# One front stage for an encoder layer on one NeuronCore: norm, input projection, forget gates and bias table merged

## Chip, core and metric

The kernel runs on one core of a Trainium2 chip, as one launch. The metric is the device time of the launch in microseconds, over repeated executions on the chip.

## What is computed

One inference step of one layer (DEPTH = 1) of a streaming encoder, for 2048 prompt rows and 8 streams of 16 new rows, so 2176 rows of 1024 values, all float32. Cut to the part that the change touches:

```python
h = rmsnorm(x, norm_mix_pre)            # x * rsqrt(mean(x*x) + 1e-6) * gain
z = h @ w_in                            # columns [qA | kA | vA | forget A (8) | qB | kB | vB], 512 each
logf = log_sigmoid(forget + b_forget)   # 8 heads
c = cumsum(logf)                        # over rows; group A adds C[t] - C[s] to its logits
# group B: chunked attention over 9 chunks of 64 with a learned bias rel_bias[h, clip(t - s)]
```

After that come the attention of both groups, the output projection and a SwiGLU feed-forward block, each with its own norm; the change leaves them alone but for what is told below. Keys, values and logf are outputs too.

## The kernel before, in words

Every float32 product is made of three float32r matmuls (`three`, L169): both operands are split into a high part (a rounded copy) and a low part (value minus high), and high x high, high x low and low x high are added up in PSUM. The work is a row of stages; each stage ends when all five engines have finished it, and a short block that clears semaphores stands ahead of the next.

- `norm_inputs` (L70) takes x, stored transposed (128 partitions x 8 feature groups x 2176 rows), in five blocks of 448 or 384 rows (`TBLK`). ScalarE squares the eight groups (L105), GpSimd adds them up (L122, L125), TensorE adds over partitions with a matrix of ones (L134), VectorE and ScalarE make 1/rms (L142, L107, L144), VectorE scales x by gain and 1/rms (L147), ScalarE copies the high part (L110) and VectorE takes the low part (L151). `xhi` and `xlo` stay in SBUF whole. There is one accumulator and the blocks follow one another.
- `project_in` (L178) takes w_in in twelve slabs of 256 columns: eight for q and k (group A and B), four for v. GpSimd makes a slab's high part (L225), VectorE its low part (L235). For q and k the slab is the stationary operand and the output is transposed: 2 x 5 groups of 24 matmuls a slab into `pz`, copied out by ScalarE (L279) and stored from ScalarE's queue. For v the rows are stationary: 17 groups of 24 matmuls a slab into `pv`, copied out at L289. The order is q and k, then v, then 120 matmuls with the 8 forget columns as stationary operand (L295 copies them out to `fT` in DRAM).
- `forget` (L304) reads fT back as 8 partitions x 2176 and runs a chain of single instructions over it, one after another: log-sigmoid (L358 to L370; ScalarE at L343 and L345), running sum (L371), sign (L372), and the running sum of the streams' stored and new values (L374, L375).
- `band_tables` (L378) reads rel_bias, extends it to 8 x 384 (L409, L410), writes it to DRAM 128 times over in eight DMAs, all from 8 partitions of SBUF (L398), and reads it back along a diagonal into `brel` (L403); two memsets on GpSimd mask its corners (L418, L420).
- `attend_prompt` (L464) begins by loading q, k, v and the bias of the first head pair (L537 to L550), splits them (L710, L712, L758, L760) and makes its first scores at L615. Its six `sums` buffers (NSM) hold the softmax sums of a job until VectorE has evicted it.

In each stage every engine has one instruction stream of its own, written out by hand, so what a stream waits for holds up all behind it. Two other stages of the kernel take 1/rms with a power on GpSimd: L1317, L1327 and L1962, `tensor_tensor(..., ALU.pow)` with an exponent of -0.5, on one or two columns of 128 partitions.

Of the kernel before, what the change touches and what calls it, by code (L numbers as in the profile page):

```python
# [9 lines left out]
ds = bass.ds  # L10
# [21 lines left out]
def f32(ap):  # L32

    return ap.bitcast(F32)
# [35 lines left out]
def norm_inputs(nc, t, xhi, xlo, keep):  # L70

    with ExitStack() as ctx:
        m = Mem(nc, ctx, "nrm", keep)
        W = 448
        x = [m.sb(f"x{u}", [P, KD, W]) for u in range(2)]
        sq = [m.sb(f"sq{u}", [P, W]) for u in range(2)]
        acc = m.sb("acc", [P, W])
        var = m.sb("var", [P, W])
        rstd = m.sb("rstd", [P, W])
        ones = m.sb("ones", [P, P])  # L80
        gain = m.sb("gain", [P, KD])
        tot = m.ps("tot", [P, 512])
        s_x = [m.sem(f"s_x{u}") for u in range(2)]
        s_gain, s_ones, s_sq, s_acc, s_tot, s_var, s_std, s_rstd, s_xn, s_hi, s_lo = (
            m.sem(n) for n in ("gain", "ones", "sq", "acc", "tot", "var", "std", "rstd", "xn", "hi", "lo"))
        with nc.Block() as block:

            @block.sync
            def _(sp):
                sp.dma_start(gain[:], t["g_pre"]).then_inc(s_gain, 16)  # L90
                for b, (t0, w) in enumerate(TBLK):
                    if b >= 2:
                        sp.wait_ge(s_lo, b - 1)
                    sp.dma_start(x[b % 2][:, :, :w], t["xT"][:, :, t0:t0 + w]).then_inc(s_x[b % 2], 16)
                sp.wait_ge(s_lo, len(TBLK))

            @block.scalar
            def _(act):
                for b, (t0, w) in enumerate(TBLK):
                    act.wait_ge(s_x[b % 2], 16 * (b // 2 + 1))  # L100
                    for k in range(KD):
                        n = b * KD + k
                        if n >= 2:
                            act.wait_ge(s_acc, n - 1)
                        nc.scalar.activation(sq[n % 2][:, :w], x[b % 2][:, k, :w], ACT.Square).then_inc(s_sq, 1)  # L105
                    act.wait_ge(s_var, b + 1)
                    nc.scalar.activation(var[:, :w], var[:, :w], ACT.Sqrt).then_inc(s_std, 1)  # L107
                    for k in range(KD):
                        act.wait_ge(s_xn, b * KD + k + 1)
                        last = nc.scalar.activation(xhi[:, k, t0:t0 + w], x[b % 2][:, k, :w], ACT.Copy)  # L110
                        last.then_inc(s_hi, 1)

            @block.gpsimd
            def _(pool):
                for b, (t0, w) in enumerate(TBLK):
                    for k in range(KD):
                        n = b * KD + k
                        pool.wait_ge(s_sq, n + 1)
                        if k == 0:
                            if b >= 1:  # L120
                                pool.wait_ge(s_tot, b)
                            nc.gpsimd.tensor_copy(acc[:, :w], sq[n % 2][:, :w]).then_inc(s_acc, 1)  # L122
                        else:
                            pool.wait_ge(s_acc, n)
                            nc.gpsimd.tensor_tensor(acc[:, :w], acc[:, :w], sq[n % 2][:, :w], ALU.add).then_inc(s_acc, 1)  # L125

            @block.tensor
            def _(pe):
                pe.wait_ge(s_ones, 1)
                for b, (t0, w) in enumerate(TBLK):  # L130
                    pe.wait_ge(s_acc, (b + 1) * KD)
                    if b >= 1:
                        pe.wait_ge(s_var, b)
                    nc.tensor.matmul(tot[:, :w], ones[:], acc[:, :w], start=True, stop=True).then_inc(s_tot, 1)  # L134

            @block.vector
            def _(dve):
                nc.vector.memset(ones[:], 1.0).then_inc(s_ones, 1)
                dve.wait_ge(s_gain, 16)
                for b, (t0, w) in enumerate(TBLK):  # L140
                    dve.wait_ge(s_tot, b + 1)
                    nc.vector.tensor_scalar(var[:, :w], tot[:, :w], 1.0 / D, EPS, ALU.mult, ALU.add).then_inc(s_var, 1)  # L142
                    dve.wait_ge(s_std, b + 1)
                    nc.vector.reciprocal(rstd[:, :w], var[:, :w]).then_inc(s_rstd, 1)  # L144
                    dve.wait_ge(s_rstd, b + 1)
                    for k in range(KD):
                        nc.vector.scalar_tensor_tensor(x[b % 2][:, k, :w], x[b % 2][:, k, :w], gain[:, k:k + 1], rstd[:, :w],  # L147
                                                       ALU.mult, ALU.mult).then_inc(s_xn, 1)
                    for k in range(KD):
                        dve.wait_ge(s_hi, b * KD + k + 1)  # L150
                        last = nc.vector.tensor_tensor(xlo[:, k, t0:t0 + w], x[b % 2][:, k, :w], f32(xhi[:, k, t0:t0 + w]),  # L151
                                                       ALU.subtract)
                    last.then_inc(s_lo, 1)


def pairs(eng, n, body):

    body(0)
    with eng.Fori(1, n) as i:
        body(i)  # L160


# [15 lines left out]
def project_in(nc, t, xhi, xlo, keep):  # L178

    CW = 256  # L180
    NZ, NV = 4 * GW // CW, 2 * GW // CW
    NS, NBK = NZ + NV, len(TBLK)
    with ExitStack() as ctx:
        m = Mem(nc, ctx, "prj", keep)
        raw = [m.sb(f"raw{u}", [P, KD, CW]) for u in range(2)]
        hi = [m.sb(f"hi{u}", [P, KD, CW], F32R) for u in range(2)]
        lo = [m.sb(f"lo{u}", [P, KD, CW], F32R) for u in range(2)]
        zo = [m.sb(f"zo{u}", [P, 448]) for u in range(NBK)]
        vo = [m.sb(f"vo{u}", [P, CW]) for u in range(2)]
        wf = m.sb("wf", [P, KD, H])  # L190
        wfh = m.sb("wfh", [P, KD, H], F32R)
        wfl = m.sb("wfl", [P, KD, H], F32R)
        pz = [m.ps(f"pz{u}", [P, 512]) for u in range(NBK)]
        pv = [m.ps(f"pv{u}", [P, 512]) for u in range(2)]
        s_raw = [m.sem(f"raw{u}") for u in range(2)]
        s_zs = [m.sem(f"z_stored{u}") for u in range(NBK)]
        s_vs = [m.sem(f"v_stored{u}") for u in range(2)]
        s_wf, s_hi, s_lo, s_z, s_ze, s_v, s_ve = (m.sem(n) for n in ("wf", "hi", "lo", "z", "ze", "v", "ve"))

        def slab_done(eng, s):  # L200

            if s < NZ:
                eng.wait_ge(s_z, (s + 1) * 2 * NBK)
            else:
                eng.wait_ge(s_v, (s - NZ + 1) * NT)

        with nc.Block() as block:

            @block.sync
            def _(sp):  # L210
                sp.dma_start(wf[:], t["w_f"]).then_inc(s_wf, 16)
                for s in range(NS):
                    if s >= 2:
                        sp.wait_ge(s_lo, s - 1 + 1)
                    sp.dma_start(raw[s % 2][:], t["w_slab"][s]).then_inc(s_raw[s % 2], 16)

            @block.gpsimd
            def _(pool):
                pool.wait_ge(s_wf, 16)
                nc.gpsimd.tensor_copy(wfh[:], wf[:]).then_inc(s_hi, 1)  # L220
                for s in range(NS):
                    pool.wait_ge(s_raw[s % 2], 16 * (s // 2 + 1))
                    if s >= 2:
                        slab_done(pool, s - 2)
                    nc.gpsimd.tensor_copy(hi[s % 2][:], raw[s % 2][:]).then_inc(s_hi, 1)  # L225

            @block.vector
            def _(dve):
                dve.wait_ge(s_hi, 1)
                nc.vector.tensor_tensor(wfl[:], wf[:], f32(wfh[:]), ALU.subtract).then_inc(s_lo, 1)  # L230
                for s in range(NS):
                    dve.wait_ge(s_hi, s + 2)
                    if s >= 2:
                        slab_done(dve, s - 2)
                    nc.vector.tensor_tensor(lo[s % 2][:], raw[s % 2][:], f32(hi[s % 2][:]), ALU.subtract).then_inc(s_lo, 1)  # L235

            @block.tensor
            def _(pe):
                def z_pair(i):
                    for u in range(2):  # L240
                        pe.wait_ge(s_lo, 2 * i + u + 2)
                        for c in range(2):
                            for b, (t0, w) in enumerate(TBLK):
                                n = ((2 * i + u) * 2 + c) * NBK + b
                                after(pe, s_ze, n - NBK + 1)
                                three(nc, pz[b][:, :w], KD,
# [13 lines left out]
                for s in range(NV):  # L260
                    v_slab(s, s % 2)
# [1857 lines left out]
```

## Time and profile before

| what | us |
|---|---|
| median of three runs | 3573.29 |
| lowest, highest | 3568.88, 3574.15 |
| the profiled execution's own time | 3568.73 |
| its span, first to last instruction | 3567.0 |
| TensorE busy (matmuls) in the span | 2971.4 |
| VectorE, ScalarE, GpSimd busy | 1632.1, 1224.0, 536.2 |

The span covers all but 1.7 us of the profiled execution's time. Busy times overlap between engines. Times in rows are microseconds from the start of the span, unless marked ns; "PEld" is TensorE's weight load, which runs beside matmuls, and a "q" behind an engine's name is its sequencer, which issues DMAs.

### The profile page before, as it was taken

Reading aid. Unit: us, or ns where it says so; the run is one execution under the profiler, and the core shown is the slowest. Engines: PE = TensorE matmul, PEld = TensorE weight load, DVE = VectorE, ACT = ScalarE, POOL = GpSimd, SP = SyncE. Lnnn points to the kernel's source line nnn. Section 1 sums busy time; section 2 is a strip of 40 time slices with the busy share of each in tenths; the row PEclk is TensorE's granted clock in tenths of the full one; section 3 lists DMA queues with packets and bytes.
Section 4 is the critical chain, followed back from the end, with each engine's and each line's share of the span. In section 5 each row is a group of like instructions: output and inputs, shape, how many; then the busy total and the mean of one; then the engine's idle time right before and its main releaser. Section 6 shows DMA issues by size and latency. Waiting matters only on the chain. (4 is left out here: it accounts for less than half of the span.)

```text
span 3567.0 us, 56750 instructions
## 1 busy us (share of the span) xinstructions
PE 2971.4 (83%) x23006; PEld 2639.4 (74%) x23006; DVE 1632.1 (46%) x3113; ACT 1224.0 (34%) x2093; POOL 536.2 (15%) x434
## 2 busy tenths in 40 slices
PE   0499999932888887745399599999999997999899
PEld 0399999922777766633278499999999996787787
DVE  4300000042677667631244477678666664323443
ACT  3211111112666666620334243343343332222221
POOL 4200000000000000000011245345434431000000
PEclk9999999976999999977799799999999998999999
DMA  2121111105022112169645432333332233434554
GB/s 96 67 72 69 71 65 53 46 16 138 26 69 71 49 48 57 51 195 295 239 131 164 140 126 97 112 99 127 107 102 97 96 112 115 122 96 119 166 168 130
DMA packets 257409, 376.35 MB, mean 106 GB/s; under 512 B 14392, under 2 KB 189552, under 8 KB 245104
## 3 DMA queue, kind: packets, MB, share of 16 engines
q1 hardware_dynamic: 235768, 346.05, 30.7%
q10 hardware_dynamic: 21392, 26.82, 2.1%
q8 instruction: 176, 2.88, 0.3%
q14 instruction: 73, 0.60, 0.1%
HBM read 283.59 MB, written 89.22 MB: 105 GB/s over the span
## 5 line engine op out<-in xcount | busy, mean ns | idle before, releaser
L1902 PE MATMUL dwn_py<-dwn_wh,dwn_ah 128*128 128x512 f32 x748 | 298.0, 398 | 42.2 <-DVE dwn_wl L1969 32.3
L1903 PE MATMUL dwn_py<-dwn_wl,dwn_ah 128*128 128x512 f32 x748 | 295.5, 395 | 0.0
L1904 PE MATMUL dwn_py<-dwn_wh,dwn_al 128*128 128x512 f32 x748 | 295.1, 395 | 0.0
L660 PE MATMUL att_po<-att_pts,att_vv 128*64 128x128 f32 x3296 | 222.7, 279 | 63.1 <-DVE att_os L812 63.1
L730 ACT ACTIVATE att_pts<-att_pt 128x384 f32<-128x384 f32 (+3 forms) x408 | 193.8, 504 | 218.2 <-PE att_pt L643 218.0
L172 PE MATMUL prj_pz<-xhi,prj_hi 128*128 128x448 f32 (+1 forms) x640 | 232.6, 363 | 22.0 <-DVE prj_lo L235 22.0
L719 ACT ACTIVATE att_sx<-att_sx,att_nm 128x640 f32<-128x640 f32 (+15 forms) x256 | 250.3, 978 | 1.3 <-DVE att_nm L786 1.3
L660 PEld LDWEIGHTS att_po<-att_pts,att_vv 128*64 128x64 f32 x3296 | 187.2, 139 | 84.1 <-issue 75.9
L235 DVE TENSOR_TENSOR prj_lo<-prj_raw,prj_hi 128x2048 fp32r<-128x2048 f32 x12 | 27.5, 2292 | 469.1 <-POOL prj_hi L225 469.1
L173 PE MATMUL prj_pz<-xlo,prj_hi 128*128 128x448 f32 (+1 forms) x640 | 232.2, 363 | 0.0
L174 PE MATMUL prj_pz<-xhi,prj_lo 128*128 128x448 f32 (+1 forms) x640 | 232.2, 363 | 0.0
L615 PE MATMUL att_s<-att_kh,att_qh 64*128 64x384 f32 (+3 forms) x544 | 116.0, 415 | 118.4 <-DVE att_ql L760 115.6
L1902 PEld LDWEIGHTS dwn_py<-dwn_wh,dwn_ah 128*128 128x128 f32 x748 | 143.3, 192 | 78.6 <-DVE dwn_al L1975 31.6
L643 PEld LDWEIGHTS att_pt<-att_eye,att_sx 64*128 64x128 f32 x3296 | 129.9, 139 | 92.8 <-ACT att_pts L730 60.1
L643 PE MATMUL att_pt<-att_eye,att_sx 64*128 64x64 f32 x3296 | 165.2, 231 | 39.0 <-DVE att_pts L797 20.6
L1622 PE MATMUL gup_z<-gup_hl,gup_wh 128*128 128x362 f32 (+1 forms) x528 | 173.5, 329 | 0.0
L1620 PE MATMUL gup_z<-gup_hh,gup_wh 128*128 128x362 f32 (+1 forms) x528 | 173.4, 328 | 0.0
L1623 PE MATMUL gup_z<-gup_hh,gup_wl 128*128 128x362 f32 (+1 forms) x528 | 172.9, 327 | 0.0
L1554 POOL TENSOR_TENSOR gup_tr<-gup_wr 128x512 f32<-128x512 f32 x66 | 89.7, 1360 | 522.5 <-DVE gup_wl L1723 391.2
L1904 PEld LDWEIGHTS dwn_py<-dwn_wh,dwn_al 128*128 128x128 f32 x748 | 143.2, 191 | 30.5
L279 ACT ACTIVATE prj_zo<-prj_pz 128x448 f32<-128x448 f32 (+1 forms) x80 | 42.8, 535 | 358.1 <-PE prj_pz L174 358.1
L1903 PEld LDWEIGHTS dwn_py<-dwn_wl,dwn_ah 128*128 128x128 f32 x748 | 143.5, 192 | 29.4
(258 smaller groups left out, 7783.8 us busy)
## 6 DMA issues: line engine op xcount, KB each, us to landing
gup_wr<-in_w_gu SPq DMA_DIRECT2D x66, 1024.0 KB, 5.3
dwn_ar<-mid_act SPq DMA_DIRECT2D x34, 1408.0 KB, 7.5
att_raw<-out_zT SPq DMA_DIRECT2D x64, 256.0 KB, 2.9
str_kr<-in_cache_ak SPq DMA_DIRECT2D x8, 2048.0 KB, 17.6
str_vr<-in_cache_av SPq DMA_DIRECT2D x8, 2048.0 KB, 15.9
mid_act<-gup_ao SPq DMA_DIRECT2D x44, 362.0 KB, 2.5
out_zT<-prj_zo ACTq DMA_DIRECT2D x64, 224.0 KB
prj_raw<-in_w_slab SPq DMA_DIRECT2D x12, 1024.0 KB, 5.1
```

Source lines behind the costliest of these rows:

```text
L172: nc.tensor.matmul(out, a_hi(k), b_hi(k), start=(k == 0), stop=False)
L173: nc.tensor.matmul(out, a_hi(k), b_lo(k), start=False, stop=False)
L174: last = nc.tensor.matmul(out, a_lo(k), b_hi(k), start=False, stop=(k == kk - 1))
L643: last = nc.tensor.transpose(pt[x][:, to:to + 64], sx[n % NSX][r, e, c:c + P], eye[r, r])
L660: last = nc.tensor.matmul(po[n % 2][r, 0:P], vv[u][:, kt, r], pts[G % NPT][:, e, j, :], start=(g == 0 and j == 0), stop=(g == len(groups) ...
L719: nc.scalar.activation(sx[n % NSX][:, e, :w], sx[n % NSX][:, e, :w], ACT.Exp, bias=nm[n % NSX][:, e:e + 1], scale=-1.0, accum_out=sums[n % ...
L730: nc.scalar.activation(pts[G % NPT][:, :, 0:k, 64 * x:64 * x + 64], pt[x][:].rearrange("p (e j q) -> p e j q", e=2, q=64)[:, :, 0:k, :], A ...
L1620: nc.tensor.matmul(out, high[:, k, :], hh[:, x, k, :w], start=(k == 0 and not more), stop=False, skip_group_check=True)
L1622: nc.tensor.matmul(out, high[:, k, :], hl[:, x, k, :w], start=False, stop=False, skip_group_check=True)
L1902: nc.tensor.matmul(out, ah[u][:, j, :], wh[:, j, :], start=(j == 0), stop=False)
L1903: nc.tensor.matmul(out, ah[u][:, j, :], wl[:, j, :], start=False, stop=False)
L1904: last = nc.tensor.matmul(out, al[u][:, j, :], wh[:, j, :], start=False, stop=(j == NJ - 1))
```

## The change

The four stages `norm_inputs`, `project_in`, `forget` and `band_tables` become one, `front`.

- x is loaded in 17 tiles of 128 rows and split raw, without norm: ScalarE copies the high part and squares (both 128 x 1024), VectorE takes the low part and adds the eight squares of a row up (`tensor_reduce`, 128 x 1024 in).
- The gain is folded into w_in as its slabs are split: ScalarE's copy and VectorE's subtraction get it as a scale, in eight pieces of 128 x 256 a slab.
- TensorE adds up over partitions twice a tile (`total`): 128 columns that hold the sum of each row along the free axis on all partitions, and 2 columns that hold it with rows on partitions. ScalarE makes mean + eps of both. GpSimd raises both to -0.5: first the column `rcol` (128 x 1), then the row `rb` (128 x 128), tile after tile in one stream.
- v comes first, the 8 forget columns as columns 256 to 263 of its first slab. A v tile is scaled by `rcol` as ScalarE copies it out of PSUM; q and k come last and are multiplied by `rb` by VectorE.
- The log-sigmoid is made on 128 x 136 while v goes on, turned to 8 partitions by 17 transposes, and summed up in four rounds of 512. The table's writes to DRAM are issued by SyncE in the second v slab.
- All stores of v, q and k are issued by SyncE, not ScalarE.
- `attend_prompt` reads the table itself behind its first loads, and GpSimd spreads and masks it there. NSM goes from 6 to 5.

The core of the diff:

```diff
+def front(nc, t, keep, neg_c):
...
             @block.sync
             def _(sp):
+                def load_x(c):
+                    if c >= NT:
+                        return
+                    if c >= NX:
+                        sp.wait_ge(s_xl, c - NX + 1)
+                        sp.wait_ge(s_sq, c - NX + 1)
+                    sp.dma_start(xr[c % NX], t["xT"][:, :, c * P:(c + 1) * P]).then_inc(s_xr[c % NX], 16)
...
+                def store_v(q, c):
+                    n = q * NT + c
+                    sp.wait_ge(s_ve, n + 1)
+                    sp.dma_start(t["v"][c * P:(c + 1) * P, q * CW:(q + 1) * CW], vo[n % 2][:]).then_inc(s_vs[n % 2], 16)
...
+                def skew():
+                    sp.wait_ge(s_ext, 2)
+                    for p in range(0, P, 16):
+                        sp.dma_start(t["skew"][:, p:p + 16, :], ext[:, None, :].to_broadcast([H, 16, EXT])).then_inc(s_skew, 16)
...
+                for c in range(NT):
+                    load_x(c + NX)
+                    if c == 2:
+                        load_raw(1)
+                    store_v(0, c)
+                tables()
+                load_raw(2)
+                for c in range(NT):
+                    store_v(1, c)
+                    if c == 4:
+                        skew()
...
             @block.gpsimd
             def _(pool):
...
+                for c in range(NT):
+                    pool.wait_ge(s_var, 2 * c + 2)
+                    nc.gpsimd.tensor_tensor(rcol[:, c:c + 1], var[:, c:c + 1], power[:], ALU.pow).then_inc(s_rc, 1)
+                    pool.wait_ge(s_rc, c + 1)
+                    row = rb[:, c * P:(c + 1) * P]
+                    nc.gpsimd.tensor_tensor(row, row, power[:].to_broadcast([P, P]), ALU.pow).then_inc(s_rb, 1)
+                    pool.wait_ge(s_rb, c + 1)
...
+                def total(c):
+                    pe.wait_ge(s_red, c + 1)
+                    if c >= NBK:
+                        pe.wait_ge(s_var, 2 * (c - NBK + 1))
+                    nc.tensor.matmul(pz[c % NBK][:, 0:P], ones[:], red[c % 2][:], start=True, stop=True, skip_group_check=True)
+                    nc.tensor.matmul(pz[c % NBK][:, P:P + 2], red[c % 2][:], ones[:, 0:2], start=True, stop=True,
+                                     skip_group_check=True).then_inc(s_tot, 1)
+
+                def v_slab(q):
...
+                    for c in range(NT):
+                        n = q * NT + c
+                        if q == 0:
+                            pe.wait_ge(s_xl, c + 1)
+                        if n >= 2:
+                            pe.wait_ge(s_ve, n - 1)
+                            pe.wait_ge(s_fe, min(n - 1, NT))
+                        three(nc, pv[n % 2][:, :w], KD,
...
+                        if q == 0:
+                            total(c)
...
+                v_slab(0)
+                v_slab(1)
+                turn_lf()
+                v_slab(2)
+                v_slab(3)
+                for q in range(NV, NS):
+                    z_slab(q)
...
+                def evict(q, c):
+                    n = q * NT + c
+                    act.wait_ge(s_v, n + 1)
+                    act.wait_ge(s_rc, c + 1)
+                    if n >= 2:
+                        act.wait_ge(s_vs[n % 2], 16 * (n // 2))
+                    nc.scalar.activation(vo[n % 2][:], pv[n % 2][:, 0:CW], ACT.Copy, scale=rcol[:, c:c + 1]).then_inc(s_ve, 1)
+                    if q == 0:
+                        nc.scalar.activation(fcol[:, c, :], pv[n % 2][:, CW:WX], ACT.Copy, scale=rcol[:, c:c + 1]).then_inc(s_fe, 1)
...
+                for c in range(NT):
+                    x_high(c + 2)
+                    variance(c)
+                    evict(0, c)
+                    if c == 12:
+                        high(1)
...
+                    nc.vector.tensor_tensor(zo[n % NZO][:, :w], pz[b][:, :w], rb[:, t0:t0 + w], ALU.mult).then_inc(s_ze, 1)
...
-    NPT, NSX, NSM, NOS, NRAW = 3, 3, 6, 4, 4
+    NPT, NSX, NSM, NOS, NRAW = 3, 3, 5, 4, 4
```

## Rows read from the trace of the kernel before

**Rows 1.** Busy time of each engine by stretch: norm, slab split, projection, gates and table, rest.

```profile
core 0: us, PE busy (x) PEld busy (x) DVE busy (x) ACT busy (x) POOL busy (x), PEclk, DMA share, GB/s
0.00:130.80 130.80, 9.06 (x10) 2.51 (x10) 62.22 (x91) 49.66 (x87) 53.57 (x44) 1.00 0.20 68
...
140.60:747.40 606.80, 606.71 (x3672) 563.72 (x3672) 25.22 (x12) 71.05 (x152) 20.75 (x11) 1.00 0.18 62
747.40:863.00 115.60, 0.00 (x0) 0.02 (x1) 47.54 (x27) 12.91 (x14) 3.80 (x10) 0.52 0.34 77
863.00:3567.00 2704.00, 2355.65 (x19324) 2073.16 (x19324) 1494.62 (x2982) 1090.38 (x1841) 454.22 (x367) 0.95 0.37 118
```

**Rows 2.** Timeline, first projection groups: first matmul, then ScalarE's copies of finished groups.

```profile
140.66 0.74 PE L172 MATMUL prj_pz<-xhi,prj_hi 128*128 128x448 f32 x1 [21.97 <-DVE prj_lo L235]
...
148.69 0.55 ACT L279 ACTIVATE prj_zo<-prj_pz 128x448 f32<-128x448 f32 x1 [21.34 <-PE prj_pz L174]
...
153.65 0.55 ACT L279 ACTIVATE prj_zo<-prj_pz 128x448 f32<-128x448 f32 x1 [4.41 <-PE prj_pz L174]
```

**Rows 3.** The v tile: min/median/max ns, first and last start; then its copy out.

```profile
L172 PE MATMUL prj_pv<-prj_hi,xhi x544: 278/283/283, 527.5 to 723.0; 128*128 128x256 f32 x182
...
L289 ACT ACTIVATE prj_vo<-prj_pv x68: 384/384/385, 530.6 to 723.6; 128x256 f32<-128x256 f32 x68
```

**Rows 4.** Timeline from projection's end to the first score.

```profile
747.92 0.27 ACTq L297 DMA_DIRECT2D mid_fT<-prj_zo  x1
749.94 0.35 SPq L326 DMA_DIRECT2D fgt_z<-mid_fT  x1
...
802.39 24.09 SPq L398 DMA_DIRECT2D mid_skew<-tab_ext  x8
...
836.08 3.66 SPq L403 DMA_DIRECT2D brel<-mid_skew  x8
...
843.62 1.76 SPq L537 DMA_DIRECT2D att_raw<-out_zT  x4
...
863.01 0.47 PE L615 MATMUL att_s<-att_kh,att_qh 64*128 64x128 f32 x2 [115.64 <-DVE att_ql L760]
```

**Rows 5.** Groups of GpSimd instructions: count, then busy, mean ns, and idle before.

```profile
L125 POOL TENSOR_TENSOR nrm_acc<-nrm_acc,nrm_sq 128x448 f32<-128x448 f32 x28 | 31.6, 1128 | 4.0
...
L1317 POOL TENSOR_TENSOR mix_r<-mix_ss,mix_power 128x2 f32<-128x2 f32 x17 | 12.0, 706 | 76.5 <-DVE mix_ss L1381 76.5
...
L1962 POOL TENSOR_TENSOR dwn_rr<-dwn_vv,dwn_power 128x1 f32<-128x1 f32 x17 | 9.2, 542 | 553.9 <-DVE dwn_vv L1992 553.9
L1327 POOL TENSOR_TENSOR mix_r<-mix_s,mix_power 128x1 f32<-128x1 f32 x17 | 9.2, 541 | 94.2 <-DVE mix_s L1406 94.2
```

**Rows 6.** Groups of TensorE, VectorE and ScalarE instructions whose shapes the change uses.

```profile
L669 PE MATMUL att_po<-att_eye,att_ot 128*64 128x128 f32 x512 | 52.9, 295 | 0.2 <-DVE att_ot L804 0.2
...
L1392 DVE TENSOR_TENSOR mix_ol<-mix_po,mix_oh 128x1024 fp32r<-128x1024 f32 x17 | 20.8, 1224 | 27.8 <-ACT mix_oh L1264 27.8
...
L1276 ACT ACTIVATE mix_j<-mix_x 128x1024 f32<-128x1024 f32 x17 | 17.9, 1052 | 6.8 <-DVE mix_x L1418 6.8
L1264 ACT ACTIVATE mix_oh<-mix_po 128x1024 fp32r<-128x1024 f32 x17 | 17.5, 1030 | 52.8 <-PE mix_po L1343 52.8
```

**Rows 7.** The table's writes to DRAM: issue time min/median/max ns.

```profile
L398 SPq DMA_DIRECT2D mid_skew<-tab_ext x8: 288/3959/4284, 802.4 to 822.4; - x8
```

**Rows 8.** DMA issues: count, KB each, median us from issue to landing.

```profile
prj_raw<-in_w_slab SPq DMA_DIRECT2D x12, 1024.0 KB, 5.1
...
out_v<-prj_vo ACTq DMA_DIRECT2D x68, 128.0 KB, 1.7
...
mix_xr<-in_x SPq DMA_DIRECT2D x17, 512.0 KB, 4.4
...
nrm_x<-in_xT SPq DMA_DIRECT2D x4, 1792.0 KB, 7.8
```

More of the change, by code:

```diff
@@ L67, in mix_rows @@
     return bass.AP(a.tensor, a.offset, [[D, TOK], [1, D]])
[L70 to L153, printed above, removed]
@@ L175, in three @@
     return last
-def project_in(nc, t, xhi, xlo, keep):
+def front(nc, t, keep, neg_c):
     CW = 256
+    WX = CW + H
     NZ, NV = 4 * GW // CW, 2 * GW // CW
     NS, NBK = NZ + NV, len(TBLK)
-    with ExitStack() as ctx:
[L184 to L188, printed above, removed]
+    NX = 3
+    NZO = 3
+    EXT = 3 * P
+    L = PAST_A + NQ
+    NR = -(-NT // 4)
+    with ExitStack() as ctx:
+        m = Mem(nc, ctx, "frt", keep)
+        xhi = m.sb("xhi", [P, KD, TOK], F32R)
+        xlo = m.sb("xlo", [P, KD, TOK], F32R)
+        shared = m.sb("shared", [P, 4 * KD * P])
+        raw = m.sb("raw", [P, KD, CW])
+        hi = [m.sb(f"hi{u}", [P, KD, WX], F32R) for u in range(2)]
+        lo = [m.sb(f"lo{u}", [P, KD, WX], F32R) for u in range(2)]
+        rb = m.sb("rb", [P, TOK])
+        red = [m.sb(f"red{u}", [P, P]) for u in range(2)]
@@ L193, in project_in, with part @@
         pz = [m.ps(f"pz{u}", [P, 512]) for u in range(NBK)]
         pv = [m.ps(f"pv{u}", [P, 512]) for u in range(2)]
-        s_raw = [m.sem(f"raw{u}") for u in range(2)]
-        s_zs = [m.sem(f"z_stored{u}") for u in range(NBK)]
-        s_vs = [m.sem(f"v_stored{u}") for u in range(2)]
[L198 to L203, printed above, removed]
-            else:
-                eng.wait_ge(s_v, (s - NZ + 1) * NT)
+        def part(a, w):
+            return shared[:, a:a + w]
@@ new lines, in front @@
+        xr = [part(u * KD * P, KD * P).rearrange("p (k t) -> p k t", k=KD) for u in range(NX)]
+        sq = part(NX * KD * P, KD * P).rearrange("p (k t) -> p k t", k=KD)
+        zo = [part(u * 448, 448) for u in range(NZO)]
+        rel = shared[0:H, 0:2 * CLIP + 1]
+        ext = shared[0:H, 260:260 + EXT]
+        fz, fe, fw, fd, lf = (part(644 + NT * H * i, NT * H) for i in range(5))
+        cs = shared[0:NB * H, 1344:1344 + L]
+        lfc, nlf, ncp = (shared[0:H, 2384 + 512 * i:2384 + 512 * (i + 1)] for i in range(3))
@@ new lines, in front @@
+        css = shared[0:NB * H, 2384:2384 + L]
+        s_xr = [m.sem(f"x{u}") for u in range(NX)]
+        s_zs = [m.sem(f"z_stored{u}") for u in range(NZO)]
+        s_vs = [m.sem(f"v_stored{u}") for u in range(2)]
+        (s_raw, s_g, s_wf, s_bf, s_c, s_wg, s_hi, s_lo, s_xh, s_xl, s_sq, s_red, s_tot, s_var, s_rc, s_rb, s_v, s_ve, s_fe, s_z,
+         s_ze) = (m.sem(n) for n in (
+             "raw", "gain", "wf", "b_forget", "consts", "wf_gained", "w_high", "w_low", "x_high", "x_low", "squares", "reduced",
+             "totals", "var", "r_column", "r_row", "v", "v_out", "f_out", "z", "z_out"))
@@ new lines, in front, with slab_done @@
+        (s_rel, s_ext, s_skew, s_st, s_act, s_lt, s_lc, s_nl, s_lfs, s_scan, s_cy, s_ncs, s_cs, s_sm, s_css) = (m.sem(n) for n in (
+            "rel_in", "extended", "skewed", "forget", "forget_act", "lf_turned", "lf_out", "lf_negated", "lf_stored", "scanned", "carry",
+            "neg_c_stored", "cache_lf", "new_lf", "csum"))
+        def slab_done(eng, q):
+            if q < NV:
+                eng.wait_ge(s_v, (q + 1) * NT)
+            else:
+                eng.wait_ge(s_z, (q - NV + 1) * 2 * NBK)
@@ L207, in project_in, with round_tiles @@
+        def round_tiles(r):
+            return list(range(4 * r, min(4 * r + 4, NT)))
         with nc.Block() as block:
@@ new lines, in _ @@
+                for q in range(NV, NS):
+                    load_raw(q + 1)
+                    for i in range(2 * NBK):
+                        store_z(q, i)
+                    if q == NV:
+                        sp.wait_ge(s_css, 2)
+                        sp.dma_start(t["csum"], css).then_inc(s_cs, 16)
+                for u in range(NZO):
+                    sp.wait_ge(s_zs[u], 16 * len(range(u, NZ * 2 * NBK, NZO)))
+                for u in range(2):
+                    sp.wait_ge(s_vs[u], 16 * (NV * NT // 2))
@@ L217, in _ @@
+                sp.wait_ge(s_skew, 16 * (P // 16))
+                sp.wait_ge(s_lfs, 16 * NR)
+                sp.wait_ge(s_ncs, 16 * (NR - 1))
+                sp.wait_ge(s_cs, 32)
             @block.gpsimd
             def _(pool):
-                pool.wait_ge(s_wf, 16)
[L220 to L225, printed above, removed]
+                nc.gpsimd.memset(power[:], -0.5).then_inc(s_c, 1)
@@ new lines, in _ @@
+                pool.wait_ge(s_c, 1)
+                nc.gpsimd.memset(ones[:], 1.0).then_inc(s_c, 1)
+                pool.wait_ge(s_c, 2)
+                nc.gpsimd.memset(eye[:], 0.0).then_inc(s_c, 1)
+                pool.wait_ge(s_c, 3)
+                nc.gpsimd.affine_select(out=eye[:], in_=eye[:], compare_op=ALU.not_equal, fill=1.0, base=0,
+                                        pattern=[[-1, P]], channel_multiplier=1).then_inc(s_c, 1)
+                pool.wait_ge(s_c, 4)
+                pool.wait_ge(s_g, 16)
@@ new lines, in low, with x_low @@
+                def low(q):
+                    if q >= NS:
+                        return
+                    dve.wait_ge(s_hi, q + 1)
+                    for k in range(KD):
+                        last = nc.vector.scalar_tensor_tensor(lo[q % 2][:, k, 0:CW], raw[:, k, :], gain[:, k:k + 1],
+                                                              f32(hi[q % 2][:, k, 0:CW]), ALU.mult, ALU.subtract)
+                    last.then_inc(s_lo, 1)
+                def x_low(c):
+                    if c >= NT:
+                        return
+                    dve.wait_ge(s_xh, c + 1)
+                    nc.vector.tensor_tensor(xlo[:, :, c * P:(c + 1) * P], xr[c % NX], f32(xhi[:, :, c * P:(c + 1) * P]),
+                                            ALU.subtract).then_inc(s_xl, 1)
+                    dve.wait_ge(s_sq, c + 1)
+                    if c >= 2:
+                        dve.wait_ge(s_tot, c - 1)
+                    nc.vector.tensor_reduce(red[c % 2][:], sq.rearrange("p k t -> p t k"), AX.X, ALU.add).then_inc(s_red, 1)
@@ new lines, in _ @@
+                dve.wait_ge(s_hi, 1)
+                nc.vector.tensor_tensor(lo[0][:, :, CW:WX], wf[:], f32(hi[0][:, :, CW:WX]), ALU.subtract)
+                low(0)
+                x_low(1)
+                for c in range(2, NT):
+                    x_low(c)
+                low(1)
+                dve.wait_ge(s_rel, 16)
+                nc.vector.tensor_copy(ext[:, 0:P - 1], rel[:, 2 * CLIP:].to_broadcast([H, P - 1])).then_inc(s_ext, 1)
+                nc.vector.tensor_copy(ext[:, P - 1:], rel[:, ::-1]).then_inc(s_ext, 1)
@@ L423 @@
+                forget()
+                low(2)
+                for r in range(NR - 1):
+                    scan(r)
+                low(3)
+                caches()
+                low(4)
+                dve.wait_ge(s_rb, NT)
+                dve.wait_ge(s_skew, 16 * (P // 16))
+                for q in range(NV, NS):
+                    for i in range(2 * NBK):
+                        z_out(q, i)
+                        if i == 3:
+                            low(q + 1)
 QB = SEQ // P
@@ L774, in biased @@
                             dve.wait_ge(s_b[u], 32 * (p // 2 + 1))
+                        if i == 0 and not fox(p):
+                            dve.wait_ge(s_brel, 3)
                         if n >= NSX:
```

410 lines of the change are left out of this document (219 added, 191 removed).

## The prediction

> **What bounds it now.** I read busy time by stretch first, then the timeline at the seams, the waits of the projection, and GpSimd's groups. The first score of the attention starts at 863.0 us; the stretches before it are what the change can move [rows 1]. Norm fills 130.8 us with every engine under half busy, and until 140.6 TensorE still waits for the first split slab. From 140.6 to 747.4 TensorE has no gap (606.71 us busy of 606.80), so there it is the bound. From 747.4 to 863.0 it does nothing for 115.6 us: gates, table, and the attention's first loads. So 140.6 + 115.6 = 256.2 us of the 863 have no projection under them, and that is the most that overlap can give.
>
> **What goes.** (a) Norm and slab split: 140.6 us. (b) Gates and table, from the last matmul at 747.4 to the attention's first DMA at 843.62: 96.2 us [rows 4]. (c) The 120 forget matmuls: v ends at 723.2 (last start 723.0 plus a matmul) and the stretch at 747.4, so 24.2 us [rows 1, 3]. Their columns ride in v slab 0, where 264 columns in place of 256 add about 3% of 49 us, 1.5 us, which lies under slab 0's other limits (below). What stays: q and k, 140.7 to 527.5, 386.8 us, of which 3 us are the slow first group (8.0 us to its copy where the next took 4.96 [rows 2]); so 384. And v: 527.5 to 723.2, 195.7 us, 68 groups of 2.88 us [rows 3].
>
> **What comes, in order of the new stage.**
>
> *Start.* The first x tile (512 KB) and slab (1 MB) load together; the nearest row for such a sum is 1792 KB in 7.8 us [rows 8], so they land near 9 us. ScalarE then takes 1.03 + 1.05 us for the tile [rows 6] and eight pieces of 128x256, 0.38 each by its copy of that size [rows 3], 3.1 us; VectorE's eight pieces behind it, at about the same, 3.4 us. First v group at 18 us, at the slow start some 5 us long; first sums and ScalarE's mean near 24 us.
>
> *Slab 0.* Four things pace a tile. TensorE: 24 matmuls of 264 columns, 2.96 us, plus two float32 matmuls; L669 is two records of 0.295 for 128 columns, overlapped, so 0.3 to 0.5 us: 3.4. ScalarE: 2.08 + mean (0.3 + 0.3) + copies out (0.38 + 0.2) = 3.3 us, plus the wait for the column's power inside its stream, 0.54 us [rows 5], and semaphores: 4.2. VectorE: low part 1.22 [rows 6], the reduction of as many elements the same: 2.5. The load of tile c+4 is issued behind the store of tile c and is due two tiles later: 4.4 us [rows 8] in two tiles, covered.
>
> The fourth is **GpSimd**, and it decides the case. Its stream is column power, row power, column power, row power; the copy out of tile c waits for column c, which stands behind row c-1, and TensorE may be only two tiles ahead. The power costs 541 ns on one column and 706 on two [rows 5]: 165 ns for a further column. The row power has 128 columns, which no row shows. From below: what the rate of an addition gives, 448 columns in 1.128 us or 2.5 ns a column, so 0.54 + 127 x 0.0025 = 0.86 us. From above: 0.541 + 127 x 0.165 = 21.5 us. I take 21.5: the only rows of this operation give the slope, and both rows repeat within some 10 ns over 17 instances. The engine's period is then 21.5 + 0.54 + 0.15 for two semaphore steps = 22.2 us, six times that of the others. Column 16 comes at 24 + 16 x 22.2 + 0.54 = 379.7 us, and TensorE resumes at 380.
>
> The Trainium skill's page "GPSIMD Engine Reference", section 3.1 ("Elementwise — side-by-side cycle accounting"), gives about 2.6 cycles an element for a two-input operation of this engine. The addition's row agrees with it (2.5 ns a column); by that rate the row power would take under 1 us and the forecast would be that of rival A. The power's own two rows speak against applying it to a power.
>
> *Rest of v.* By then one group of slab 1 is done (two PSUM buffers). 50 groups x 2.88 = 144 us; the clock has to come back after slab 0, as at the start: 3 us.
>
> *Table's writes.* SyncE issues eight DMAs behind store (1,4). Before, issuing took 24.09 us (3959 ns median for one [rows 7]) and the last landed at 836.08, 33.7 us after the first began [rows 4]. Store (1,5) stands behind them in the same queue and lands some 35 us after store (1,4) was issued. With two v buffers in SBUF and two in PSUM, TensorE goes on for four groups, 11.5 us, then waits 24 us; its clock restart adds 3. I take 27. Bounds: 0 if the DMA engines serve the store between, 35 if nothing goes on.
>
> *Gates.* The chain shrinks from 8 x 2176 to 128 x 136 and runs under v; 17 transposes at about 0.22 us: 4 us on TensorE. The four rounds of running sums wait for DMAs of about 2 us within ScalarE's and VectorE's streams, in slab 2, under the same two-buffer slack: 0, at most 5. Splitting later slabs costs 3.1 and 3.4 us on either engine against 49 us a slab: 0. VectorE's product with `rb` takes about 0.62 us of a 4.95 us group: 0. Slab loads, 5.1 us, are issued a slab ahead: 0.
>
> *Tail.* Last group copied out 0.6, stored and landed about 2.5, seam 0.4; then the attention's start as before, 863.0 - 843.6 = 19.4: 23 us. The table's reads stand behind those loads; reading took at most 7.5 us before (836.1 to 843.6 [rows 4]) and the band heads come hundreds of us later: 0. If that cover fails, 7.5. One `sums` buffer less makes ScalarE wait for an eviction once at each of the seven changes of head pair, 0.3 us each: 2, between 0 and 7.
>
> **Sum.** 380 + 144 + 3 + 27 + 4 + 384 + 23 = 965 us to the first score, against 863: 102 later, and 2 in the attention. The profiled execution's own time is 3568.7 (span 3567.0 and 1.7 around it), so 3672.7, that is 2.9% slower. The median of the runs shown is 4.6 above the profiled time, so the error of that base is small. A measurement of this kernel can tell about 0.2%, 7 us, from no change.
>
> **Rivals.**
>
> *A. The row power is cheap, and all overlaps* (the other side). Below about 3.5 us for a row, GpSimd is out of the way and ScalarE paces slab 0: 18 + 17 x 4.2 = 89; 51 groups 147; then 27 + 4 + 384 + 23: 674 to the first score, 189 earlier; with 2 back, 3382. For it: two rows cannot tell a per-column cost from a rest loop's that longer shapes avoid, and the addition shows that this engine can stream. Against: the slope. Chance 0.2.
>
> *B. Partly cheaper*: long shapes treat columns several at a time, 4 to 15 us a row. Every us of row power is worth 16 us. Break-even is where 16 x (21.5 - T) = 104, T = 15.0 us or 114 ns a column. At a quarter of the slope (41 ns) the row takes 5.8, the period 6.5, column 16 comes at 128: first score 713, time 3421. Chance 0.2, nearly all of it on the faster side, 0.02 within 0.2%.
>
> *C. Table's writes cost nothing* beside a slow power: stores slip between them. 27 less: 3646. Slower still, inside my forecast's own range.
>
> *D. The change shifts but does not hide*: the row power slows VectorE through their shared SBUF access. VectorE needs 2.5 of 22 us, so there is room; not priced.
>
> Forecast as stated (row power at 18 us or more), C and D within it: 0.60.
>
> **Range.** Forecast's own: 3640 (no stall for the table) to 3690 (stalls at their bounds). With both signs holding most of the chance, the 8-in-10 range must reach to A and B: 3375 to 3690. Faster 0.38 (A 0.2, B 0.18), same 0.02, slower 0.60.
>
> **What would show it.** Right: a 128x128 power on GpSimd of about 21 us x17; ScalarE's copy out of v waiting for GpSimd for over 250 us in total; TensorE near 15% busy from 24 to 380 us at the low clock; a gap of over 20 us in v slab 1 ended by a store; first score near 965. Wrong: a row power under 15 us, which turns the sign; slab 0 done by 100 us with ScalarE busy throughout is A.

## The result, and the profile after

The changed kernel takes 3661.61 us in the median of four runs (3653.15 to 3668.9), against 3571.09 us for the kernel before, run beside it. The ratio is 1.0258, with a 95% interval of 1.0236 to 1.028: slower by 2.6%. The forecast was 3672.7 us, with 3640 to 3690 as its own range and 3375 to 3690 as the range over all cases. The profiled execution took 3660.78 us; its span is 3659.1 us, 92.1 more than before.

First the busy time of each engine by stretch, in the columns of [rows 1]. The stretches are: to the first v group, the slow first slab, the rest of v in two parts, q and k, and the attention's start.

```profile
core 0: us, PE busy (x) PEld busy (x) DVE busy (x) ACT busy (x) POOL busy (x), PEclk, DMA share, GB/s
0.00:16.70 16.70, 0.00 (x0) 0.01 (x1) 6.51 (x12) 9.46 (x15) 1.31 (x9) 1.00 0.68 191
...
23.00:366.00 343.00, 86.79 (x463) 85.65 (x461) 47.17 (x37) 43.31 (x100) 340.49 (x32) 0.61 0.10 29
...
382.00:442.40 60.40, 35.39 (x278) 35.18 (x277) 6.01 (x16) 6.91 (x14) 4.75 (x1) 0.77 0.32 53
442.40:540.80 98.40, 98.40 (x836) 98.03 (x835) 14.98 (x25) 26.23 (x59) 0.00 (x0) 1.00 0.21 69
540.80:920.80 380.00, 380.00 (x1923) 355.70 (x1921) 70.48 (x135) 23.65 (x57) 0.00 (x0) 1.00 0.19 68
```

The stretch from 23 to 366 is new. GpSimd is busy for 340.49 of 343.00 us, TensorE for 86.79 at a mean granted clock of 0.61 (the column PEclk), VectorE and ScalarE for less than 48 each. This is one slab of v; in the kernel before a slab of v took 49 us with TensorE full. The groups of GpSimd's two powers, in the columns of [rows 5]:

```profile
L273 POOL TENSOR_TENSOR frt_rb<-frt_rb,frt_power 128x128 f32<-128x128 f32 x17 | 352.6, 20741 | 1.3
...
L270 POOL TENSOR_TENSOR frt_rcol<-frt_var,frt_power 128x1 f32<-128x1 f32 x17 | 9.3, 549 | 15.1 <-ACT frt_rb L361 13.8
```

With [rows 5] this gives three widths of the same operation: 549 ns for 1 column (541 before), 706 for 2, 20741 for 128. From 1 to 128 it is (20741 - 549) / 127 = 159 ns a column; from 1 to 2 it was 165. Nothing in the wide shape is cheaper.

How this reaches TensorE is seen in the timeline at the end of slab 0:

```profile
344.56 20.74 POOL L273 TENSOR_TENSOR frt_rb<-frt_rb,frt_power 128x128 f32<-128x128 f32 x1
344.56 0.47 ACT L370 ACTIVATE frt_vo<-frt_pv,frt_rcol 128x256 f32<-128x256 f32 x1 [20.59 <-issue]
...
345.34 0.55 PE L79 MATMUL frt_pv<-frt_hi,frt_xhi 128*128 128x256 f32 x1 [16.43 <-ACT frt_fcol L372]
...
365.38 0.55 POOL L270 TENSOR_TENSOR frt_rcol<-frt_var,frt_power 128x1 f32<-128x1 f32 x1
366.00 20.74 POOL L273 TENSOR_TENSOR frt_rb<-frt_rb,frt_power 128x128 f32<-128x128 f32 x1
366.01 0.47 ACT L370 ACTIVATE frt_vo<-frt_pv,frt_rcol 128x256 f32<-128x256 f32 x1 [20.58 <-issue]
366.38 0.26 ACT L372 ACTIVATE frt_fcol<-frt_pv,frt_rcol 128x8 f32<-128x8 f32 x1
...
366.78 0.55 PE L79 MATMUL frt_pv<-frt_hi,frt_xhi 128*128 128x256 f32 x1 [15.99 <-ACT frt_fcol L372]
```

The row power ends, the column power follows, and within 0.1 us of its end ScalarE copies the v tile out and frees the PSUM buffer for which TensorE has waited 16 us. The period is 366.00 - 344.56 = 21.44 us. The trace puts ScalarE's wait down to "issue"; that its copy starts as the column power ends is what names the releaser. Only two of its waits, 19.5 us, are credited to GpSimd outright; the other fifteen, 281.0 us, stand under "issue".

The second loss, in the groups of waits between 0 and 970 us (who waited for whom: total us, times, longest), and the table's writes, in the columns of [rows 7]:

```profile
ACT frt_vo L370 <- DMA out_v<-frt_vo: 32.4, 2, 27.8
...
PE frt_pv L79 <- ACT frt_vo L370: 25.0, 1, 25.0
```

```profile
L194 SPq DMA_DIRECT2D mid_skew<-frt_shared x8: 337/3902/4164, 382.2 to 402.2; - x8
```

SyncE issues the eight writes from 382.2 to 406.3 and the next v store at 406.4. ScalarE, which needs that store's buffer, goes on at 416.6: it has waited 27.8 us for the store's landing, and TensorE 25.0 us for ScalarE. So the store is late twice: it is issued 24 us late, and it lands 10.2 us after its issue, where the median v store takes 1.8.

The end of the new stage, against [rows 4]:

```profile
921.42 0.33 SPq L183 DMA_DIRECT2D out_zT<-frt_shared  x1
...
923.76 1.77 SPq L642 DMA_DIRECT2D att_raw<-out_zT  x4
...
942.94 2.74 POOL L709 COPY att_brel<-att_far 128x3072 f32<-128x3072 f32 x1 [15.91 <-DMA att_far<-in_rel_bias]
...
943.26 2.97 DVE L879 SCALAR_TENSOR_TENSOR att_ql<-att_raw,att_qh 128x512 fp32r<-128x512 f32 x1 [0.36 <-ACT att_qh L831]
...
946.38 0.47 PE L734 MATMUL att_s<-att_kh,att_qh 64*128 64x128 f32 x2 [25.58 <-DVE att_ql L879]
```

So the change did what it says: the 115.6 us without matmuls ahead of the attention became 25.6, and norm's 140.6 us became 16.7. These 214 us, and the 24 of the forget matmuls, were spent again in slab 0, and more. The first score comes at 946.4 instead of 863.0, 83.4 us later. Of the other 8.7 us of the span, 6.6 lie in the prompt's attention, from first score to last eviction (863.0 to 1546.4 before, 946.4 to 1636.4 after), where the waits between 863 and 1620 us show

```profile
ACT att_sx L838 <- DVE att_os L933: 16.4, 7, 2.6
```

in place of none: seven waits, one at each change of head pair. The last 2.1 us lie behind the attention; nothing was run on them.

### The profile page after: what moved, and what is told of

Same layout as the page of the kernel before. It is cut to its first block and busy times, and to the rows that moved or that the text cites. A ratio compares the mean times of both kernels' runs of the same rounds, so it can differ in the third digit from the quotient of the medians.

```text
span 3659.1 us, 56595 instructions
## 1 busy us (share of the span) xinstructions
PE 2979.6 (81%) x22961; PEld 2667.3 (73%) x22961; DVE 1654.0 (45%) x3224; ACT 1214.4 (33%) x2112; POOL 823.5 (23%) x421
## 5 line engine op out<-in xcount | busy, mean ns | idle before, releaser
L79 PE MATMUL frt_pv<-frt_hi,frt_xhi 128*128 128x256 f32 (+1 forms) x544 | 172.9, 318 | 298.7 <-ACT frt_fcol L372 257.0
L273 POOL TENSOR_TENSOR frt_rb<-frt_rb,frt_power 128x128 f32<-128x128 f32 x17 | 352.6, 20741 | 1.3
L79 PEld LDWEIGHTS frt_pv<-frt_hi,frt_xhi 128*128 128x128 f32 x544 | 119.4, 220 | 300.2 <-issue 258.5
L838 ACT ACTIVATE att_sx<-att_sx,att_nm 128x640 f32<-128x640 f32 (+15 forms) x256 | 250.3, 978 | 20.1 <-DVE att_os L933 16.4
L79 PE MATMUL frt_pz<-frt_xhi,frt_hi 128*128 128x448 f32 (+1 forms) x640 | 230.5, 360 | 0.0
L81 PE MATMUL frt_pz<-frt_xhi,frt_lo 128*128 128x448 f32 (+1 forms) x640 | 230.5, 360 | 0.0
L80 PE MATMUL frt_pz<-frt_xlo,frt_hi 128*128 128x448 f32 (+1 forms) x640 | 230.0, 359 | 0.0
L494 DVE TENSOR_TENSOR frt_shared<-frt_pz,frt_rb 128x448 f32<-128x448 f32 (+1 forms) x80 | 48.9, 611 | 339.2 <-PE frt_pz L81 339.2
L370 ACT ACTIVATE frt_vo<-frt_pv,frt_rcol 128x256 f32<-128x256 f32 x68 | 32.0, 472 | 428.2 <-issue 281.0
```

Source lines behind the costliest of these rows:

```text
L79: nc.tensor.matmul(out, a_hi(k), b_hi(k), start=(k == 0), stop=False)
L80: nc.tensor.matmul(out, a_hi(k), b_lo(k), start=False, stop=False)
L81: last = nc.tensor.matmul(out, a_lo(k), b_hi(k), start=False, stop=(k == kk - 1))
L273: nc.gpsimd.tensor_tensor(row, row, power[:].to_broadcast([P, P]), ALU.pow).then_inc(s_rb, 1)
L838: nc.scalar.activation(sx[n % NSX][:, e, :w], sx[n % NSX][:, e, :w], ACT.Exp, bias=nm[n % NSX][:, e:e + 1], scale=-1.0, accum_out=sums[n % ...
```

## The experiments

The theory: GpSimd's row power, in the stream ahead of the next column power, paces slab 0; the table's writes cost a gap of their own; the missing sums buffer costs the rest. The rivals: another engine or the x loads pace slab 0; the writes cost the same however they are issued; the attention is longer because of the table's reads and spreading. Each experiment changes one thing, or puts together what was changed one by one before. They ran in two sets of four, each beside 17 runs of the kernel before on the same chip: medians 3569.81 us (columns first, row by square root, writes one at a time, five buffers before) and 3570.18 us (the rest).

### Column powers first

```diff
                 for c in range(NT):
                     pool.wait_ge(s_var, 2 * c + 2)
                     nc.gpsimd.tensor_tensor(rcol[:, c:c + 1], var[:, c:c + 1], power[:], ALU.pow).then_inc(s_rc, 1)
                     pool.wait_ge(s_rc, c + 1)
+                for c in range(NT):
                     row = rb[:, c * P:(c + 1) * P]
```

> The changed kernel with one edit on GpSimd: all 17 column powers first, then the 17 row powers. Main theory (the row powers of 20.74 us, standing in the stream ahead of the next column power, pace slab 0): slab 0 then runs at ScalarE's pace, near 4.3 us a tile, and ends near 90 us; the rows take 17 x 20.8 = 354 us from there and end near 445, and the q and k products wait for them. TensorE finishes v near 265 us (25 of it behind the table's writes) but its q and k groups stop after five until 445. First score near 445 + 380 + 26 = 851, in place of 946: about 95 us less than the changed kernel, 3566 us. Rival (another engine or the x loads pace slab 0 and the power only fills the time): no more than 10 us less than the changed kernel, 3650 or over. Rival (GpSimd's long instructions slow VectorE through SBUF so far that moving them gives nothing back): VectorE's splits in v slabs 1 to 3 take over twice their 0.48 us.

Measured: 3544.74 us, ratio 0.9931 (0.9914 to 0.9948): 117 us less than the changed kernel, by moving instructions within one stream, and 0.7% faster than the kernel before. Its two powers (columns of [rows 3]), and its waits between 0 and 900 us:

```profile
L270 POOL TENSOR_TENSOR frt_rcol<-frt_var,frt_power x17: 548/549/803, 22.3 to 90.3; 128x1 f32<-128x1 f32 x17
...
L274 POOL TENSOR_TENSOR frt_rb<-frt_rb,frt_power x17: 20715/20717/20738, 90.9 to 423.6; 128x128 f32<-128x128 f32 x17
```

```profile
DVE frt_shared L495 <- POOL frt_rb L274: 209.6, 1, 209.6
...
PE frt_pz L79 <- DVE frt_shared L495: 156.7, 1, 156.7
```

Slab 0 ends at 91 us: (90.3 - 22.3) / 16 = 4.25 us a tile. The last row is ready at 423.6 + 20.7 = 444.3, and now the products with the row wait there. In this place the rows keep TensorE waiting 157 us; in the other they stretched slab 0 from 4.25 to 21.44 us a tile. The expectation was 21 us too high, for a reason that it names and doesn't subtract: TensorE has five groups of about 4.8 us done and waiting in PSUM when the rows are ready (first score at 828.4, expected 851). The rival of a slowed VectorE falls: its 96 splits of a slab piece take 476 to 486 ns, whether or not a row power runs beside them.

### The row by square root and reciprocal

```diff
                     pool.wait_ge(s_rc, c + 1)
-                    row = rb[:, c * P:(c + 1) * P]
-                    nc.gpsimd.tensor_tensor(row, row, power[:].to_broadcast([P, P]), ALU.pow).then_inc(s_rb, 1)
-                    pool.wait_ge(s_rb, c + 1)
...
+                    if c == 10:
+                        act.wait_ge(s_var, 2 * NT)
+                        nc.scalar.activation(rb[:], rb[:], ACT.Sqrt).then_inc(s_rb, 1)
...
-                dve.wait_ge(s_rb, NT)
+                dve.wait_ge(s_rb, 1)
+                nc.vector.reciprocal(rb[:], rb[:]).then_inc(s_rb, 1)
+                dve.wait_ge(s_rb, 2)
```

> The changed kernel with the row power taken off GpSimd: ScalarE takes the square root of the whole row of mean + eps (128 x 2176) in the second v slab, VectorE its reciprocal (about 14 us) after its last split of the v part, both under TensorE's work; the column power stays. Main theory: slab 0 runs at 4.3 us a tile and ends near 90 us; v 51 groups of 2.84 = 145, the stall behind the table's writes 25, turns 2, q and k 380, tail 26: first score near 668 in place of 946, so about 3383 us, 5% below the kernel before. Rival (ScalarE, with copy, square, mean and copies out of each tile, is slower than its 4.3 us a tile, or x tiles come late): slab 0 at 6 us a tile or more, 3410 us or over. Rival (the power isn't what costs): within 1% of the changed kernel.

Measured: 3385.58 us, ratio 0.9482 (0.9465 to 0.95). The whole row costs what these two lines show (columns of [rows 3]), both under matmuls, and the column powers run as in the experiment above. The line behind them is slab 0, in the columns of [rows 1]:

```profile
L406 ACT ACTIVATE frt_rb<-frt_rb x1: 2023/2023/2023, 151.4 to 151.4; 128x2176 f32<-128x2176 f32 x1
L517 DVE RECIPROCAL frt_rb<-frt_rb x1: 13741/13741/13741, 235.0 to 235.0; 128x2176 f32<-128x2176 f32 x1
```

```profile
17.00:92.50 75.50, 65.20 (x487) 64.58 (x488) 52.31 (x40) 45.84 (x104) 9.59 (x17) 0.95 0.45 133
```

That is 15.8 us of two engines for all 2176 columns, against 352.6 of GpSimd. The 276 us between this kernel and the changed one are the cost of the row power where it stood: the first score comes at 670.2, expected 668. Slab 0 takes 4.3 us a tile, so the rival by which other engines or the x loads are much slower than that falls, and so does the one by which the power isn't what costs. That ScalarE alone paces slab 0 now isn't shown: TensorE has matmuls for 65 of the 75 us, and between 17 and 91 us ScalarE waits in seven waits, 8.3 us together, for x. The stall behind the table's writes is still there: 25.2 us in one wait of TensorE.

### The table's writes, one at a time

```diff
-                    if c == 4:
-                        skew()
+                    if c >= 4 and c % 2 == 0:
+                        skew(c // 2 - 2)
...
+                    if c == 1:
+                        skew(7)
```

(in slabs 1 and 2; `skew(i)` issues one of the eight writes)

> The changed kernel with the eight writes of the bias table to DRAM no longer issued in a block after v tile 4 of the second slab, but one behind every second v store. Main theory (the block holds SyncE 24 us and the stores behind it 35, which two v buffers can't bridge): the 25.0 us gap on TensorE in v slab 1 goes and each single write of about 4.2 us delays one store by less than the slack: 25 us less, about 3636 us. Rival (the writes slow every transfer beside them, however they are issued): the same 25 us are lost in smaller gaps, 3655 us or over.

Measured: 3638.0 us, ratio 1.0186 (1.017 to 1.0202): 23.6 us less than the changed kernel. Issuing a write no longer holds SyncE:

```profile
L194 SPq DMA_DIRECT2D mid_skew<-frt_shared x8: 332/337/1139, 383.2 to 424.5; - x8
```

The same eight writes are issued within 42 us instead of 24, and the 25.0 us wait of TensorE is gone; the first score comes at 921.1, 25.3 us earlier. So it was the block of writes ahead of a store that cost, not the bytes.

### Both repairs

> Both repairs in one: the row by square root and reciprocal, and the table's writes one behind every second v store. If the two costs are separate, as the main theory has it, the 25.2 us gap of the row repair alone goes too: about 3386 - 24 = 3362 us. If the writes slow whatever runs beside them once v is no longer held up by anything else (rival), under 10 us of it come back: 3376 us or over.

Measured: 3359.41 us, ratio 0.9407 (0.9389 to 0.9424): 26.2 less than with the row repair alone. The two losses add up, so they were separate. Between slab 0 and the end of q and k, TensorE is now without matmuls for only 1.1 us (columns of [rows 1]: slab 0, the rest of v, q and k):

```profile
17.00:92.20 75.20, 63.59 (x496) 62.91 (x496) 51.94 (x40) 46.66 (x105) 9.61 (x17) 0.98 0.45 134
92.20:239.00 146.80, 145.71 (x1227) 144.88 (x1227) 35.58 (x46) 42.34 (x89) 0.00 (x0) 1.00 0.31 82
239.00:618.00 379.00, 379.00 (x1917) 354.87 (x1916) 70.43 (x135) 23.17 (x56) 0.00 (x0) 1.00 0.19 68
```

### Five sums buffers in the kernel before

```diff
-    NPT, NSX, NSM, NOS, NRAW = 3, 3, 6, 4, 4
+    NPT, NSX, NSM, NOS, NRAW = 3, 3, 5, 4, 4
```

> The kernel before with one number changed: five softmax sum buffers in place of six. Theory from the changed kernel's trace (ScalarE waits 16.4 us in seven waits for VectorE's evictions, 2.3 us at each change of head pair, and its attention from first score to last eviction is 6.6 us longer): 5 to 8 us more than before, ratio near 1.002. Rival (those 6.6 us come from the table's reads and GpSimd's spreading of the table, which now run within the attention): under 2 us more, ratio 1.0005 or less.

Measured: 3577.03 us over twelve runs, ratio 1.0023 (1.0014 to 1.0032): 7.2 us more. In the attention it shows the seven waits of the changed kernel, which the kernel before doesn't have:

```profile
ACT att_sx L719 <- DVE att_os L812: 16.5, 7, 2.6
```

### Six sums buffers in the repaired kernel

```diff
-        far = m.sb("far", [P, H])
+        far = bb[1][:, 0, 0:H]
...
-    NPT, NSX, NSM, NOS, NRAW = 3, 3, 5, 4, 4
+    NPT, NSX, NSM, NOS, NRAW = 3, 3, 6, 4, 4
```

(the load of the second bias waits until the spreading has read `far`)

> The last kernel with six softmax sum buffers again (room is made by keeping the 128 x 8 column of far biases in the second bias buffer, which is loaded later). Theory from the kernel before with five (8 us more): 6 to 8 us less than the last, about 3355 us, and ScalarE's seven waits of 2.3 us for evictions gone. Rival (here the attention's time is set by something else that changed): no difference over 2 us.

Measured: 3349.67 us, ratio 0.9385 (0.937 to 0.94), 9.7 less than with five. The seven waits are gone, and the attention takes 682.6 us from first score to last eviction (642.6 to 1325.2). The 9.7 us are above the 6 to 8 expected, but the runs of the kernel with five spread over 12 us, so what lies above 8 isn't shown to be the buffer's. Over all ten traces the attention takes 682.6 to 683.4 us in the four kernels with six buffers and 690.0 to 694.9 in the six with five. Two of the four with six read and spread the table within the attention. So the 6.6 us are the buffer's, not the table's.

### The spreading of the table later

```diff
                 pool.wait_ge(s_far, 16)
+                pool.wait_ge(s_ex, 4)
```

> The last kernel with GpSimd's spreading of the table (128 x 3072, 2.74 us) held back until two jobs of the attention have been through the exponential. Theory (the copy lengthens VectorE's last split of q from 0.69 to 2.97 us, right ahead of the first score): 2.3 us earlier to the first score, and at most 2 us less in all, since VectorE's work on the following jobs meets the copy in its place. Rival (the split is long for another reason): it stays at 2.97 us.

Measured: 3349.5 us, ratio 0.9378 (0.9363 to 0.9393): no difference to the last. The split behaves as the theory says: among the 32 splits of q the longest is now 693 ns, where it was 2975:

```profile
L886 DVE SCALAR_TENSOR_TENSOR att_ql<-att_raw,att_qh x32: 679/681/693, 640.2 to 1252.6; 128x512 fp32r<-128x512 f32 x32
```

From the last store of q and k to the first score it is 22.7 us (620.8 to 643.5) in place of 24.0 (618.6 to 642.6). That is 1.3 us of the 2.3 expected: in this execution ScalarE's first split of q started 16.4 us after the first load's issue, in place of 15.5, and took most of the rest. The 1.3 us are too little for the runs to show.

### The slab loop of the kernel before written out

```diff
-    body(0)
-    with eng.Fori(1, n) as i:
+    for i in range(n):
         body(i)
```

> The kernel before with the hardware loop over pairs of q and k slabs written out, nothing else. It asks why the same q and k products take 380.0 us in the changed kernel and 386.8 before (3 of it a slow start). If the loop is the reason: 3 to 4 us less than before and the spacing of matmuls of 448 columns falls from 206 ns. If it is not (rival: which engine copies out, or where x lies in SBUF), no difference over 1 us and the same spacing.

Measured: 3567.69 us over twelve runs, ratio 0.9993 (0.9984 to 1.0003): no difference that can be told. From first to last start the q and k matmuls take 385.5 us, against 386.3 before and 379.2 in the changed kernel, so their spacing has hardly moved. Their median duration stays at 368 ns, as before, where the changed kernel has 363. The loop is not the reason; what makes the same products 1% quicker in the new stage, beyond the 3 us of the slow start, stays open.

## Why the prediction was right

The likeliest case, given a chance of 0.60, came true by its mechanism, and 11.1 us high (3672.7 forecast, 3661.61 measured). In the profiled execution (3660.78) the first score comes 18.6 us before the 965 forecast; 4.6 us more in the attention than the 2 forecast and 2.1 behind it, for which the sum has no term, take part of that back. Term by term:

- **Start**, 18 us: 16.7. The first x tile lands at 7.7 rather than 9.
- **Slab 0**, the step that decided the sign. The choice was between 0.86 and 21.5 us for a row power that no row showed, and 21.5 was taken because the only two rows of the operation gave the slope. It measured 20.74, the period 21.44 for 22.2, and column 16 came at 366.0 for 379.7. These 14 us are most of what the sum to the first score is off. Exactly two points, a column apart, carried the extrapolation to 128; a slope 4% off was good luck as well as sound. The two-column rows don't repeat within the 10 ns that the prediction says: their 17 instances go from 690 to 716 ns, and 10 ns in the slope are 1.3 us in the row power. Another slip changes nothing: 22.2 us is 5.3 times ScalarE's 4.2, not six times.
- **TensorE in slab 0**, forecast near 15% busy: 99.0 of the 356 us from 24 to 380, 28%. The forecast took 3.4 us a tile, from rows at full clock; at the granted clock of 0.61 it was 86.79 us in 16 periods, 5.4 a tile. This reading was wrong and cost nothing, since 16 us of waiting were left. ScalarE's waits for the column power came to 300.5 us, as forecast (over 250).
- **Rest of v**, 144 + 3 + 27 + 4 = 178 us from there: 540.8 - 366.8 = 174.0. The table's writes, taken at 27 between 0 and 35, left a wait of 25.0 and a granted clock of 0.68 for 6 us after it (419 to 425); spreading them gave 23.6 back.
- **q and k**, 384: 380.0.
- **Tail**, 23: 25.6. What failed here is "the attention's start as before", 19.4: it took 22.6 (923.8 to 946.4). The sum has a term for the table's reads, 0, but none for the spreading on GpSimd, which meets VectorE's last split and makes it 2.97 us in place of 0.69. That is 2.3 of the 3.2 us; whether the reads have a part in the other 0.9 isn't shown.
- **Attention**, 2 with 0 to 7 as bounds: 6.6, and 7.2 for the same edit alone. The mechanism was right, down to the seven changes of head pair. The size was off: each makes ScalarE wait 2.3 us, not 0.3, of which about 1 us reaches the total.
- **Rivals.** A's time, 3382, was that of a cheap row power, and the kernel whose row is cheap takes 3385.58; its slab 0 takes 4.3 us a tile for the 4.2 assumed. The x loads, taken as covered, aren't quite at that pace (8.3 us of waits). B falls with the three widths. C, writes that slip between the stores and cost nothing, didn't come true (25.0 us of waiting); they do slip through where they are issued one by one. D: VectorE's reduction took 1.94 us where 1.22 was assumed, and lay under GpSimd's time. It takes as long with the row power gone (1.94 us in the mean), so that is its strided read or the operation itself, and not the power beside it. Nor does the power slow VectorE's subtraction, whose two inputs both lie in SBUF. It takes 1.21 to 1.23 us in all 17 tiles, also in the middle of a row power:

```profile
22.87 20.75 POOL L273 TENSOR_TENSOR frt_rb<-frt_rb,frt_power 128x128 f32<-128x128 f32 x1
...
24.50 1.23 DVE L435 TENSOR_TENSOR frt_xlo<-frt_shared,frt_xhi 128x1024 fp32r<-128x1024 f32 x1 [0.67 <-ACT frt_xhi L353]
```

On the Trainium skill's 2.6 cycles an element ("GPSIMD Engine Reference", section 3.1): the trace doesn't agree for this operation. The row power measured 20.74 us, and an estimate by the page's rate gives under 1. The page states it for an addition, where [rows 5] bear it out, and the measurement decides that it isn't a rate for a power.

## What to carry to other kernels

Before an operation is moved to a larger shape, read its cost at two sizes in the trace: a cost per column that is invisible at one column (0.55 us) can be the whole stage at 128. Look at what stands behind a long instruction in its own stream: against the kernel where two other engines make the row in 15.8 us of hidden work, the same 17 row powers cost 276 us ahead of the column powers (3661.61 - 3385.58) and 159 behind them (3544.74 - 3385.58). The idea of the change was worth having: repaired in three places, it takes 3349.67 us, 6.2% less than the kernel before.

## What the runs showed of the hardware

- GpSimd's power costs 159 to 165 ns a column of 128 partitions at widths of 1, 2 and 128, some sixty times the 2.5 ns of its addition. VectorE's reciprocal is 13.74 / 2176 = 6.3 ns a column.
- A GpSimd copy of 2.74 us that overlapped a VectorE operation on SBUF operands stretched it from 0.69 to 2.97 us: begun at 943.3, it ended at 946.2, 0.55 us behind the copy's end. With the copy moved away, it was 0.69 again. GpSimd's power of 20.74 us did nothing of the kind to VectorE operations with two SBUF inputs (1.23 us beside it, 1.22 without).
- Eight DMAs of 192 KB, all read from 8 partitions, hold their queue for some 4 us each: a store behind them landed 34.4 us after the first was issued (382.2 to 416.6). An issuing engine that sends them in a block is itself held for 24 us; sent one by one between stores, each issue takes 0.34 us in the median.
- TensorE's granted clock was 0.61 of full in the mean over slab 0, nearer the lower of its two levels of 1.2 and 2.4 GHz, where it worked about 5 us of every 21.4. There it cost nothing, since GpSimd set the pace.
